# Feed-forward stage of a hybrid encoder layer: both matrices by Strassen-Winograd products, rectified values and stream kept in DRAM

## What is computed

```python
    h = rmsnorm(x, norm_ffn)
    x = x + jnp.square(jax.nn.relu(h @ w_ffn1)) @ w_ffn2      # 1024 -> 4096 -> 1024
...
y_prompt = rmsnorm(xp, norm_final)
y_sample = rmsnorm(xs, norm_final)
```

## Time and profile before

| | |
|---|---|
| median of 3 runs | 1810.17 us (1808.38 to 1810.33) |
| profiled execution, its own time | 1809.99 us |
| its span (first to last instruction) | 1808.0 us |
| mean granted TensorE clock | 0.993 |
| feed-forward stage | from 997.73 us to the end |

### The profile page before, as it was taken

One profiled execution on the slowest core, in us unless ns is written; L12 is line 12 of the kernel. 1 busy time (PEld: TensorE's weight loads), 2 busy tenths in 40 slices (PEclk: granted clock), 3 DMA queues, 4 the chain that ended last, 5 costly groups with the idle time before them and its releaser, 6 DMA issues. The chain is left out here.

```text
span 1808.0 us, 24870 instructions
## 1 busy us (share of the span) xinstructions
PE 1753.9 (97%) x10398; PEld 1563.6 (86%) x10398; DVE 942.9 (52%) x1307; ACT 689.5 (38%) x986; POOL 34.1 (2%) x49
## 2 busy tenths in 40 slices
PE   9999999999999989999989999999999999999998
PEld 8777777889999978789878989889898989899896
DVE  6577778566776798454455433333233332323334
ACT  5577777653443565123553311112030211211122
POOL 1000000000000001000000000000000000000001
PEclk9999999999999989999999999999999999999999
DMA  5322122110111243612430111111111111111102
GB/s 184 91 64 75 47 75 75 48 49 24 49 54 31 72 149 103 229 47 71 120 103 24 59 47 36 36 57 37 47 41 30 59 36 47 44 39 36 47 24 105
DMA packets 147936, 118.02 MB, mean 65 GB/s; under 512 B 4593, under 2 KB 129137, under 8 KB 147826
## 3 DMA queue, kind: packets, MB, share of 16 engines
q1 hardware_dynamic: 147826, 116.44, 20.9%
HBM read 98.40 MB, written 18.02 MB: 64 GB/s over the span
## 5 line engine op out<-in xcount | busy, mean ns | idle before, releaser
L227 ACT ACTIVATE sbuf_w_hi<-sbuf_raw 128x1024 fp32r<-128x1024 f32 x116 | 121.7, 1053 | 379.6 <-PE PS L2193 315.5
L2147 PE MATMUL PS<-sbuf_h_hi,sbuf_w_hi 128*128 128x384 f32 x768 | 256.9, 334 | 0.0
L2149 PE MATMUL PS<-sbuf_h_hi,sbuf_w_lo 128*128 128x384 f32 x768 | 256.6, 334 | 0.0
L2148 PE MATMUL PS<-sbuf_h_lo,sbuf_w_hi 128*128 128x384 f32 x768 | 256.6, 334 | 0.0
L2245 DVE TENSOR_TENSOR sbuf_X<-PS,sbuf_X 128x512 f32<-128x512 f32 x144 | 99.5, 691 | 251.6 <-PE PS L2193 251.4
L2192 PE MATMUL PS<-sbuf_w_hi,sbuf_u_lo 128*128 128x512 f32 x576 | 227.2, 395 | 0.0
L2193 PE MATMUL PS<-sbuf_w_lo,sbuf_u_hi 128*128 128x512 f32 x576 | 227.2, 395 | 0.0
L2191 PE MATMUL PS<-sbuf_w_hi,sbuf_u_hi 128*128 128x512 f32 x576 | 227.2, 394 | 0.0
L567 PE MATMUL PS<-sbuf_h_hi,sbuf_w_hi 128*128 128x384 f32 x600 | 212.7, 355 | 6.1 <-ACT sbuf_g_N L578 2.7
L569 PE MATMUL PS<-sbuf_h_hi,sbuf_w_lo 128*128 128x384 f32 x600 | 202.5, 338 | 0.0
L568 PE MATMUL PS<-sbuf_h_lo,sbuf_w_hi 128*128 128x384 f32 x600 | 202.5, 337 | 0.0
(11 more groups left out here) (269 smaller groups left out, 2867.2 us busy)
## 6 DMA issues: line engine op xcount, KB each, us to landing
sbuf_raw<-w_ffn SPq DMA_DIRECT2D x64, 512.0 KB, 4.0
sbuf_raw<-w_in SPq DMA_DIRECT2D x28, 512.0 KB, 4.8
sbuf_X<-x_prompt SPq DMA_DIRECT2D x16, 512.0 KB, 7.3
sbuf_s_cK<-cache_sb_k SPq DMA_DIRECT2D x8, 512.0 KB, 4.6
sbuf_s_cV<-cache_sb_v SPq DMA_DIRECT2D x4, 1024.0 KB, 7.9
sbuf_raw<-w_out SPq DMA_DIRECT2D x8, 512.0 KB, 4.2
out_yp<-sbuf_X SPq DMA_DIRECT2D x8, 512.0 KB, 2.6
sbuf_r_lo<-mixT SPq DMA_DIRECT2D x7, 576.0 KB, 9.1
```

What stands on the lines that cost most here:

```text
L227: act.activation(w_hi[s][:], raw[s % 2][:], ACT.Copy).then_inc(cut_hi[s % 2], 1)
L2147: pe.matmul(out, hi, h_hi[:, kb, tok], start=kb == 0, stop=False)
L2148: pe.matmul(out, hi, h_lo[:, kb, tok], start=False, stop=False)
L2149: last = pe.matmul(out, lo, h_hi[:, kb, tok], start=False, stop=kb == KB - 1)
```

## The change

Every half-size block product is done by the Winograd form of Strassen's algorithm: seven products of half-size operands and some additions in place of eight products.

- First matrix, in 16 units of 256 features. The tokens are split into two halves of 576 (`HT`), the model dimension into two halves of 512, the 256 features into two of 128. The left-hand sums S1 to S4 of the normalised tokens are made once and kept, high and low parts, in SBUF; of the right-hand side VectorE makes T1 to T4 for each unit (`f_blocks`). A product is 4 (`KH`) x 3 matmuls for each of two quarters of 288 tokens (`QT`), 24 matmuls. Partial results are taken from PSUM by ScalarE (P1, P6, P7, P4) into a buffer `f_ub`, and by VectorE's additions (`out_of`). Products are interleaved over two units (`ff_step`).
- The rectified, squared values of a unit (2 x 1152 words a partition) and the three sums that the second matrix needs (`sums`, 3 x 512 words) are stored to DRAM (`store_u`, 1.18 and 0.79 MB). The stream X is stored to DRAM (`xD`) before the first matrix and loaded again before the second.
- Second matrix, after the first is complete, in 4 turns of 1024 features. The 1024 prompt tokens are split into two halves of 4 tiles, the output columns into two of 512, the features into two interleaved halves. A product is 4 pieces (`GU`) x 4 tiles x 3 matmuls of 512 columns; the sample tile ("S") is multiplied in the ordinary way beside four of the seven products of a turn, in all 28 products and 1536 matmuls. The operand u of a product (1.05 MB) is loaded from DRAM (`u_unit`) and cut into high and low parts piece by piece, as the weights are, in rings of six (`RING`).
- `final` handling leaves the shared norm helper and is written out in the last products, for tiles 4 to 7, the sample tile, 0 to 3.

In the excerpt `Since` objects are old semaphores counted on from where they stand; `f_p` counts TensorE's products (pieces, later), `f_cp` ScalarE's copies, `f_ev` VectorE's additions, `f_st` stores, `f_u` finished units. `w_high`/`w_low` and `u_high`/`u_low` cut one piece of 512 words a partition.

```diff
...
+        A_OF = {"P1": "A11", "P2": "A12", "P3": "S4", "P4": "A22", "P5": "S1", "P6": "S2", "P7": "S3"}
...
+        def ff_step(n):
+            if n == 0:
+                return [("P5", 0), ("P6", 0), ("P7", 0), ("P4", 0), ("P3", 0)]
+            if n == UNITS - 1:
+                return [("P6", n), ("P5", n), ("P7", n), ("P4", n), ("P3", n)]
...
...
+        PAIR = {"P1": (6, 2), "P6": (6, 2), "P7": (6, 2), "P4": (6, 2), "P2": (4, 4), "P5": (0, 0), "P3": (0, 0)}
...
+            elif k - RING < NFF:
+                eng.wait_ge(f_p, k - RING + 1)
+            else:
+                eng.wait_ge(f_p, STEP[k - RING - NFF])
...
+            eng.wait_ge(f_in[k % 2].sem, f_in[k % 2].n(16 * (UNITS // 2 + k // 2 + 1)))
+            if q < 2:
+                eng.wait_ge(f_p, FF_AT["P5", LASTU] + 1)
+            elif q < 4:
+                eng.wait_ge(f_p, FF_AT["P7", LASTU] + 1)
+            elif q < RING:
+                eng.wait_ge(f_st[0], 32 * (UNITS // 2))
+            else:
+                eng.wait_ge(f_p, STEP[q - RING])
...
+        U_EARLY = {NFF - 4: (0, 1), NFF - 3: (2, 3), NFF - 2: (4,), NFF - 1: (5,)}
...
+                        dve.wait_ge(xl[done], 48)
+                    dve.tensor_tensor(a_raw["S1"][:, :, tok], a_raw["S1"][:, :, tok], ff_psum(t, 1, cols), ALU.add)
+                    dve.tensor_tensor(a_raw["S3"][:, :, tok], a_raw["A11"][:, :, tok], ff_psum(t, 0, cols),
+                                      ALU.subtract).then_inc(N["lo"], 1)
+                    dve.tensor_tensor(a_lo["A22"][:, :, tok], ff_psum(t, 1, cols),
+                                      a_hi["A22"][:, :, tok].bitcast(F32), ALU.subtract).then_inc(N["lo"], 1)
...
+        def mo_behind(dve, p):
+            if p == 0:
+                f_blocks(dve, 0)
+                w_low(dve, 0)
+                w_low(dve, 1)
...
+        def f_blocks(dve, n):
...
+            b12 = w_block("T1", n)
...
+            dve.wait_ge(f_t, 4 * n + T_AT["T2"])
...
+                if what == "P1":
+                    if n == 0:
+                        pe.wait_ge(mo_s[1], 2 * NT - 1)
+                        pe.wait_ge(N["lo"], 2 * (n_ff.base + 5))
+                    elif n == 1:
+                        pe.wait_ge(N["lo"], 2 * (n_ff.base + NT - 1))
+                        pe.wait_ge(f_cp, CP["P4", n - 2])
+                if what == "P2":
+                    if n == 0:
+                        pe.wait_ge(mo_s[1], 2 * NT)
+                        pe.wait_ge(f_ev, EV["X11", n - 1])
+                if what == "P5":
+                    if n == 0:
+                        pe.wait_ge(N["lo"], 2 * (n_ff.base + NT))
+                    else:
+                        pe.wait_ge(f_ev, EV["X12", n - 1])
+                if what == "P6":
+                    pe.wait_ge(f_cp, CP["P1", n])
+                if what == "P7":
+                    pe.wait_ge(f_cp, CP["P6", n])
+                if what == "P4":
+                    pe.wait_ge(f_cp, CP["P7", n])
+                if what == "P3":
+                    pe.wait_ge(f_ev, EV["X22", n])
+                if n == 0 and what in SUM_AT:
+                    pe.wait_ge(a_low.sem, a_low.n(SUM_AT[what]))
+                pe.wait_ge(w_cut_lo.sem, w_cut_lo.n(s + 1))
+                hi, lo = w_op(s, 0), w_op(s, 1)
+                x_hi, x_lo = a_hi[A_OF[what]], a_lo[A_OF[what]]
+                first = what in ("P1", "P2", "P5")
+                for q in range(2):
+                    out = pair(what, n)[:, q, :]
+                    tok = slice(q * QT, (q + 1) * QT)
+                    for kb in range(KH):
+                        pe.matmul(out, hi[:, kb, :], x_hi[:, kb, tok], start=first and kb == 0, stop=False,
+                                  skip_group_check=True)
+                        pe.matmul(out, hi[:, kb, :], x_lo[:, kb, tok], start=False, stop=False,
+                                  skip_group_check=True)
+                        last = pe.matmul(out, lo[:, kb, :], x_hi[:, kb, tok], start=False,
+                                         stop=kb == KH - 1, skip_group_check=True)
+                last.then_inc(f_p, 1)
...
+                    act.wait_ge(f_p, s + 1)
+                    x = f_part(n, {"P1": 0, "P6": 2, "P7": 3, "P4": 1}[what])
+                    if what == "P1":
+                        if n >= 2:
+                            act.wait_ge(f_st[n % 2], 32 * (n // 2))
+                        else:
+                            for done in range(4 + 2 * n, 7 + 2 * n):
+                                act.wait_ge(xl[done], 48)
+                    act.activation(x, pair(what, n), ACT.Relu if what == "P4" else ACT.Copy).then_inc(f_cp, 1)
+                    if what == "P4":
+                        act.wait_ge(f_cp, CP[what, n])
+                        act.activation(x, x, ACT.Square).then_inc(x_sq.sem, 1)
+                if s == 1:
+                    act.wait_ge(N["lo"], 2 * (n_ff.base + NT))
+                    sum_high("S1", 0)
+                if s == 2:
+                    act.wait_ge(a_sum.sem, a_sum.n(1))
+                    sum_high("S2", 1)
+                    sum_high("S3", 2)
+                if s == 3:
+                    act.wait_ge(a_sum.sem, a_sum.n(2))
+                    sum_high("S4", 3)
+                w_high(act, s + RING)
+                for q in U_EARLY.get(s, ()):
+                    u_high(act, q)
+            s_high(act, 0, 0)
+            s_high(act, 0, 1)
...
+            def out_of(what, n):
+                i, ends, left = {"X11": (0, "P2", "P1"), "X22": (3, "P5", "P7"), "X12": (2, "P3", "P6")}[what]
+                dve.wait_ge(f_p, FF_AT[ends, n] + 1)
+                dve.wait_ge(f_cp, CP[left, n])
+                dve.tensor_tensor(f_part(n, i), pair(ends, n), f_part(n, i), ALU.add).then_inc(f_ev, 1)
+                dve.wait_ge(f_ev, EV[what, n])
...
+                od.then(squared(f_part(n, i)))
+                dve.wait_ge(x_sq.sem, x_sq.n(n + 1))
+                sums(n)
+            def sums(n):
+                u = f_ub[n % 2]
+                a11, a21, a12, a22 = (u[:, x:x + HS] for x in (0, HS, T, T + HS))
+                if n:
+                    dve.wait_ge(f_st[(n - 1) % 2], 32 * ((n - 1) // 2 + 1))
+                od.then(dve.tensor_tensor(f_S[:, 0, :], a21, a22, ALU.add))
+                dve.tensor_tensor(a21, a11, a21, ALU.subtract)
+                od.then(dve.tensor_tensor(f_S[:, 1, :], f_S[:, 0, :], a11, ALU.subtract))
+                dve.tensor_tensor(f_S[:, 2, :], a12, f_S[:, 1, :], ALU.subtract).then_inc(f_u, 1)
+            w_low(dve, 4)
+            w_low(dve, 5)
+            for s, (what, n) in enumerate(FF):
+                if outs_after(s):
+                    out_of(*outs_after(s))
+                if s == 1:
+                    dve.wait_ge(N["lo"], 2 * (n_ff.base + NT))
+                    dve.tensor_tensor(a_raw["S2"], a_raw["S1"], a_raw["A11"], ALU.subtract).then_inc(a_sum.sem, 1)
+                    sum_low("S1", 0)
+                if s == 2:
+                    dve.wait_ge(a_sum.sem, a_sum.n(1))
+                    dve.tensor_tensor(a_raw["S4"], a_raw["A12"], a_raw["S2"], ALU.subtract).then_inc(a_sum.sem, 1)
+                    dve.wait_ge(a_sum.sem, a_sum.n(2))
+                    sum_low("S2", 1)
+                if s == 3:
+                    sum_low("S3", 2)
+                    f_blocks(dve, 1)
+                    sum_low("S4", 3)
+                if n >= 1 and n + 1 < UNITS and s == FF_STEP[n]:
...
+                for q in U_EARLY.get(s, ()):
+                    u_low(dve, q)
+            s_low(dve, 0, 0)
+            s_low(dve, 0, 1)
...
+                g, i = divmod(k, 7)
+                if t == "S":
+                    pe.wait_ge(g_s_lo.sem, g_s_lo.n(2 * g + (1, 2, 0, 0, 0, 1, 2)[i]))
+                    if i == 0:
...
+                elif i == 0:
+                    pe.wait_ge(f_ev, ADD[k - 3, t] if t < 3 else ADD[k - 1, "S"])
...
+                    u_hi, u_lo = (g_so[:, 0 if k % 7 in (0, 5) else 1, half_, kb, :] for half_ in range(2))
+                else:
...
+                    for h in range(2):
+                        blocks(g, ("T3", "T2")[kb], h)
+                if q + RING < NPC:
+                    w_low(dve, NFF + q + RING)
+                    u_low(dve, q + RING)
+                if g + 1 < TURNS and kb == 0 and i == 6:
...
+            def pair_unit(n):
+                sp.dma_start(f_raw[n % 2], w1[:, :, n * 2 * P:(n + 1) * 2 * P]).then_inc(f_in[n % 2].sem, 16)
+            def store_u(n):
+                sp.wait_ge(f_u, n + 1)
+                sp.dma_start(uD[:, n, 0:2 * T], f_ub[n % 2]).then_inc(f_st[n % 2], 16)
+                sp.dma_start(uD[:, n, 2 * T:UW].rearrange("p (a b) -> p a b", a=3), f_S).then_inc(f_st[n % 2], 16)
...
+            def u_unit(k):
+                g, i = divmod(k, 7)
+                stored(g)
+                if k >= 2:
+                    sp.wait_ge(u_cut_lo.sem, u_cut_lo.n(GU * (k - 1)))
```

(31 more changed lines are left out.)

818 lines of the change are left out of this document (588 added, 230 removed).

## The result

The changed kernel takes 1763.89 us (median of 4 runs, 1762.61 to 1765.91) against 1810.06 us (4 runs, 1808.38 to 1810.33) beside it: ratio 0.9748, 95% interval 0.9731 to 0.9765, 46 us or 2.5% faster. The profiled execution took 1764.4 us, with 1762.4 us of span. The prediction was 1761, range 1740 to 1798.

A forecast was written before the change was run, and what follows sets the result against it. TensorE, busy 97% of the span, was taken as the bound. From 1809.99 us, -85.7 + 11.4 + 0.9 + 16.3 + 4.4 + 4.0 + 0.2 = -48.5 gave 1761.5, stated as 1761, range 1740 to 1798.

The forecast's parts named there:

- likeliest case: Whole kernel: the forecast outcome, a time of 1748 to 1776 us; chance 0.45.
- First matrix, pitch: First matrix: 2688 matmuls of 288 columns start every 133.4 ns, 358.5 us in all, saving 41.1 us.
- That rival: Feed-forward matmuls: weight loads are not hidden, 192 more of 188 ns add 36 us, giving 1797 us; chance 0.02.
- Second matrix, pitch: Second matrix: 1536 matmuls of 512 columns against 1728, at the old 232.3 ns, 356.8 us, saving 44.6 us.
- Start: First nine products: TensorE waits for VectorE's chain before P5, P6, P7 of unit 0, +11.4 us.
- Steady unit: First-matrix units: chain from store to X22 leaves 1.0 us margin before P3, so 0 us added, bounds 0 to +2 each.
- second rival: First-matrix units: the 1.0 us margin is missing, each unit takes 1 to 2 us more, 1775 to 1790 us; chance 0.22.
- Change-over: Between the matrices: queued DMA loads hold ScalarE and VectorE, TensorE waits 11.4 us, then 4.6 and 0.3, together +16.3 us.
- Clock: Start and the two waits between the matrices: TensorE runs at 1.2 GHz after each wait, +4.4 us.
- Inside the second matrix: Second matrix: additions just in time at product ends, two delayed 0.7 us by T4 and T1, +4 us in all.
- smooth change-over: Between the matrices: loads land in time, +3.4 us instead of +16.3 and no slow clock there, 1745 us; chance 0.17.
- The store as the bound at half rate: First-matrix units: DRAM writes run at half the read rate, the store lands 4.9 us later, 1816 us; chance 0.09.

The follow-up runs named there:

- e8: Kernel before the change, second-matrix matmuls taking their stationary operand from the normed stream (20.8 kB) instead of the squared values: 1798.34 us against 1808.51.
- e11: Kernel before the change, each of eight groups of second-matrix loops taking its stationary operands from another tensor, mapping pitch by place: 1805.76 us, one run.
- e7: Changed kernel, but at the start ScalarE cuts the weights of the tenth and eleventh product behind its copy of P6 of unit 0: 1760.51 us.
- e6: Changed kernel, but the three sums of every unit are stored twice, and whoever waits for a store waits for the copy too: 1802.92 us.
- e12: e10 plus 72 already fulfilled waits in TensorE's program before P5 of unit 0, shifting instruction fetches against the weight loads: 1733.55 us.
- e1 to e4: Four reorderings of the changed kernel's change-over: engine order 1761.45 us, DMA order 1752.96, both 1750.85, both with sample tiles split still earlier 1751.00.
- e4: Changed kernel with DMA and engine orders changed at the change-over, sample tiles split before the last unit's X12 block and sums: 1751.00 us.
- e10: Changed kernel with change-over reordered as in e4, store split, start reordered, third stream load earlier, T4 and T1 block sums later: 1735.43 us.

## Why the prediction was right, and where its terms were off

Predicted and measured parts of the stage, from 997.73 us as in the earlier trace rows (the slow clock's 4.4 us put where the waits are: 1.5 at the start, 2.9 in the second matrix):

| part | predicted | measured | off |
|---|---|---|---|
| start, to the ninth product's end | 43.5 | 45.4 | +1.9 |
| other 103 products, last unit's wait | 330.7 | 333.2 | +2.5 |
| second matrix to the last matmul | 380.0 | 378.4 | -1.6 |
| tail | 7.4 | 7.6 | +0.2 |
| sum (before: 810.3) | 761.6 | 764.6 | +3.0 |

So 48.5 us were forecast and 45.6 measured in the profiled execution. The likeliest case came true and its mechanism is the one described, but that the sum is so close is partly luck. The two pitches were 10.6 us too dear (2.3 and 8.3 below); with them right the same sum gives 1751. P1 0 was forecast about 1 us later than the first matmul of the stage before, at 998.7, and started at 996.18, 2.5 us sooner; the first row hides this, the start itself took 46.98 us where 42.5 were forecast. Against these 13.1 us stand waits, slow clock and restarts that were some 16 us too cheap.

- **First matrix, pitch.** 132.5 ns for 133.4: -2.3 us over 2688. The rate taken from 256 and 384 columns carried over. The Trainium skill's rule that a weight load is hidden only behind another row group (TensorE: Matmul & The Clock Gate, The mechanism, in Part 3; the same section also lets a load into the background weight buffer go ahead) is not borne out: loads last 188 to 191 ns and matmuls start every 132.5 ns, so that even a load longer than the whole pitch is hidden. That rival is out.
- **Second matrix, pitch: the term that was mis-sized.** 1536 matmuls at 226.9 ns, not 232.3: 348.5 us for 356.8. I took the old pitch over because the shape stayed; e8 and e11 show that it came from where the stationary operand lay (185.0 and 203.5 kB of a partition), and the change happens to put the new stream ring at 140 to 167 kB. About 8 us of what the change gains have nothing to do with Strassen: e8 gets 10 us without it. Why that place costs 5.5 ns a matmul no run shows.
- **Start.** P5, P6 and P3 of unit 0 were forecast at 1018.7, 1024.4 and 1036.5, measured 1016.7, 1022.4 and 1040.0. The sums of VectorE's operations were right: 8.2 us from the last tile's cut to the low part of S1 and 5.7 from P5 to P6, as counted. They came 2 us early because the last tile was cut at 1008.4, not 1010.5. What failed is P7. I had it wait for VectorE's chain alone, and missed that ScalarE's copy of P6 stood behind a weight cut that needs a VectorE block sum of the next unit: 4.59 us. e7 takes the queue position away and the start shrinks by 4.5.
- **Steady unit.** The margin, counted at 1.0 us, is there in two of three units and used up in the third, whose load is 1.5 us later and whose wait is 0.8 to 1.0. The prediction's chain (store, load behind it, cuts, X11, X22) is the right one, as e6 shows by its price, and the second rival's slips happened, but 4 of 14 and not every unit: +3.6 us and the restarts (the first matmul behind such a wait starts 0.24 us ahead of the second, not 0.13). The slip comes with an instruction fetch on the DMA engines, which no step of the prediction had; e12 moves the fetches and the slips go.
- **Last unit.** 0.74 for 0.9.
- **Change-over.** 13.24 for 11.4 and 4.64 for 4.6, in the places and behind the calls named (`u_high(4)`, `u_low(8)`). The first is longer because `u_unit(1)` landed 8.6 us behind the first matrix's end where about 7 were counted. From 1364.00, when the store of unit 14 is issued, to that landing at 1384.93 the DMA engines are full (busy share 1.01 as the profile counts it); 353 GB/s pass, 7.4 MB and not 6.7, since the loads of X issued from 1376.24 on share the end of it. e1 to e4 confirm the account piece by piece, and add what it did not say: the wait is held up in two queues, and freeing one only uncovers the other. The Trainium skill's limit of about 358 GB/s (DMA: Bandwidth & Descriptors, Specifications) lies just above this mean, but stretches of 2 us in it pass 387 to 408 GB/s, over the limit like the 404 of the earlier trace rows.
- **Clock.** In the stretch of 0.50 quoted above (1.2 of 2.4 GHz) 9 of the matmuls behind the first wait start 0.43 us apart instead of 0.227, 1.9 us lost; about 2.1 are lost behind the second. At the start P5 of unit 0 loses 1.4 us, which only shortens the wait before P6, and P7 behind its wait of 4.59 us loses 2.2. That is 7.6 for 4.4. Three places were foreseen; the start has 10.2 us at half clock, not 3.4.
- **Inside the second matrix.** Waits of 4.1 us for 4.0. The stretch holds about 4 us more, spread over the first matmuls behind the 13 waits, which I have not split up. e10 shows that T4 and T1 were the cause at its place: with the same edits otherwise the second matrix is 4.6 us shorter.
- **Rivals.** The smooth change-over was priced at 1745. e4, built for it, gives 1751, since its wait moved on into the second product; e10 gets the change-over down to 2.8 us. The store as the bound at half rate is out as a fact: the store of the blocks lands in 4.2 us, the sums in 6.2. Its mechanism is sound: e6 lengthens the store and comes within 0.4% of the time before. The second rival came true in part, as said under the steady unit, with 4.6 us (waits and restarts) in place of 14 to 28.
